# Scatters ahead of gathers in the expert loop of a mixture-of-experts layer on one Trainium2 core

## The chip, the cores and the metric

The kernel runs on one core of a Trainium2 chip. The time is the device time of one execution in microseconds (us). Engines: PE is TensorE, DVE is VectorE, ACT is ScalarE, POOL is GpSimd, and SP is SyncE, which here only issues DMAs and passes semaphores on. All engines run their own instruction lists in order and meet at semaphores.

## The reference

One transformer layer over 512 latent tokens of width 1024 with 256 context tokens: modulated normalisation, one input projection that feeds differential attention (4 heads) and a centred pooling group, an output projection, and then a mixture of experts. All of it is float32. The part that matters here is the last:

```python
scores = sigmoid(t @ w_router)                      # 512 tokens, 64 experts
wts, top_e = 8 experts per token (4 of 8 groups), weights normalised, times 2.5
yb = swiglu(x_of_slot, w_e_gate[e], w_e_up[e], w_e_down[e]) * slot_weight   # 1024 -> 256 -> 1024
routed = segment_sum(yb, slot_tok)                  # 8 rows per token
x = x + g_f * rmsnorm(routed + shared, g_post_ffn)
```

With the inputs drawn, the experts get between 1 and 265 tokens. In blocks of at most 64 tokens of one expert that makes 103 blocks; the first 62 experts (index 0 to 61) fill blocks 0 to 100, the expert with index 62 has block 101 and the last one block 102.

## The kernel before

**Stages.** Up to about 370 us the kernel does the layer's first half, the routing and the shared expert, and builds tables of which token stands in which slot. Then comes a loop over passes. A pass p takes two blocks of 64 slots (a pair, 128 rows), blocks 2p and 2p + 1. There are 52 passes; the count is computed at run time. At the end the four tiles of 128 tokens are summed, normalised and stored.

**What one pass needs.** Each step runs on another engine, and several passes are in flight:

- GpSimd gathers the pair's 128 token rows from DRAM into `xg[q]` (q is p % 2) with four indirect DMAs, 256 columns each (`gather`, L577, the DMA at L581). It takes its row indices from `gidx[:, q]`.
- VectorE turns the block, `turn_block` (L1756, instruction L1758), into `xT[:, q]`. It waits for the gather (`s_gt[q]`) and counts `s_xte`.
- TensorE multiplies with the gate and up weights, `gate_up` (L1274, 32 matmuls in two column halves of the array, one for each block of the pair). The second block's weights come from `cur_g`, which VectorE copies (`copy_gate_up`, L1754) once SyncE has counted the weights' arrival (`s_w`, L465).
- ScalarE applies SiLU (`block_silu`, L897), VectorE multiplies with the up half and the slot weights (`gated`, L1786), TensorE transposes the hidden rows (`turn_hidden`, L1297), VectorE keeps them (`keep_hidden`, L1792), TensorE multiplies with the down weights (`down`, L1286). The second block's down weights are a copy by ScalarE in `cur_d` (`copy_down`, L832).
- ScalarE copies the result out of PSUM into `ysb[:, q]` (`keep_y`, L893). For that it waits until the scatter of two pairs earlier, which read the same buffer, has landed (`s_scat[q]`).
- GpSimd scatters the 128 rows to DRAM with two indirect DMAs (`scatter`, L585): L588 writes rows, L591 adds rows to what stands there. It takes its indices from `sidx[:, q]`.

**Order on the engines.** TensorE in pass p: `turn_hidden` of p - 1, `gate_up` of p, `down` of p - 1. VectorE in pass p: turn the block of p + 1, `gated` of p, copy gate and up weights for p + 1, `keep_hidden` of p. ScalarE in pass p (`open_pass`, `close_pass`): the gather indices for p + 2 (`gather_index`, L834, behind a wait for the transpose of p), SiLU of p, `keep_y` of p - 1, the scatter indices of p - 1 (`scatter_index`, L838), `copy_down` for p. GpSimd in each step: the four gathers of p + 2, then the two scatters of p - 2. All six go through GpSimd's one DMA queue (q0).

**Weights.** SyncE loads one expert after the other (3 MB each) into a ring of 6 places (7 for the down weights), `load_gate_up` and `load_down`. Before a load it waits for the arrival of the expert two before it, and for the last matmul that uses the place (L524, L452).

**The end.** The last passes are written out. In them pass 50's `gate_up` follows `down` of 49. The last two pairs are not scattered: TensorE folds them into the tiles (`fold`, L1380) from `ysb`. When all scatters have landed, SyncE loads each tile's four partial sums (L542), VectorE adds them (`add_sums(t)`, three additions, L1825 to L1827), adds the folded rows (`add_rows`, L1851), and multiplies (`finish`, L1862 or L1865); ScalarE computes the norm in between (L955). In the last pass (k == -1) `add_sums(0)` stands in front of `keep_hidden`, whose copy the last `down` waits for.

Of the kernel before, what the change touches and what calls it, by code (L numbers as in the profile page):

```python
# [48 lines left out]
LEAST = E // 2  # L49
# [63 lines left out]
def build(nc, a, hbuf, sums, out):  # L113
    with ExitStack() as ctx:
# [82 lines left out]
        arow = rows[:, :].rearrange("p (r n) -> p r n", r=4)  # L197
# [31 lines left out]
        ysb = xres[:, 2:4, :]  # L229
# [324 lines left out]
        def _(pool):  # L554
# [22 lines left out]
            def gather(p, q, set_by):  # L577
                pool.wait_ge(s_gi, set_by)
                pool.sem_inc(s_pgo, 1)
                for s in range(4):  # L580
                    pool.indirect_dma_start(xg[q][:, 256 * s:256 * s + 256], None, hrows,  # L581
                                            bass.IndirectOffsetOnAxis(gidx[:, q, s:s + 1].bitcast(U32), 0),
                                            bounds_check=4 * T - 1, oob_is_err=False).then_inc(s_gt[q], 16)

            def scatter(p, q, rows_of_pair, indices_set):  # L585
                pool.wait_ge(s_si, indices_set)
                pool.sem_inc(s_pgo, 1)
                pool.indirect_dma_start(sums, bass.IndirectOffsetOnAxis(sidx[:, q, 0:1].bitcast(U32), 0),  # L588
                                        rows_of_pair, None, bounds_check=PARTS * T - 1, oob_is_err=False)\
                    .then_inc(s_scat[q], 16)  # L590
                pool.indirect_dma_start(sums, bass.IndirectOffsetOnAxis(sidx[:, q, 1:2].bitcast(U32), 0),  # L591
                                        rows_of_pair, None, bounds_check=PARTS * T - 1, oob_is_err=False,
                                        compute_op=ALU.add).then_inc(s_scat[q], 16)
# [15 lines left out]
            gather(1, 1, 1)  # L609
            pool.wait_ge(s_adre, 8)  # L610
            for p in range(2):
                gather(p + 2, p, p + 2)
                scatter(p - 2, p, arow[:, 3], p + 1)
            for t in range(NT):
                pool.wait_ge(s_sh_st[t], 16)
            pool.wait_ge(s_tab, 1)
# [1 line left out]
            more = pool.snap((extra + 3) // 4)  # L618
            last = pool.snap(more * 2 + (LEAST - 2))
            with pool.Fori(2, last, 2) as i:  # L620
                for q in range(2):
                    gather(i + (q + 2), q, i + (q + 2))
                    scatter(i + (q - 2), q, ysb[:, q], i + (q + 1))
            for q in range(2):
                n_set = pool.snap(more * 2 + (LEAST - 1 + q))
                scatter(None, q, ysb[:, q], n_set)
# [13 lines left out]
        def _(act):  # L640
# [184 lines left out]
            def down_weights(p):  # L825
                e = act.value_load(tab[0:1, bass.ds(p * 2 + 3, 1)], min_val=0, max_val=E - 1)
                return e, act.snap(((e + 1) % ND) * EW + 2 * CW)

            def copy_down(e, w0):
                act.wait_ge(s_wdn, e + 2)  # L830
                for j in range(FJ):
                    act.copy(cur_d[:, j, :], wring[:, bass.ds(w0 + j * D, D)]).then_inc(s_cdn, 1)  # L832

            def gather_index(p, q):  # L834
                act.wait_ge(s_xte, p - 1)
                act.copy(gidx[:, q, :], slot_g[:, bass.ds((p + 1) * 4, 4)]).then_inc(s_gi, 1)

            def scatter_index(p, q):  # L838
                act.copy(sidx[:, q:q + 1, :], slot_idx[:, bass.ds(p + 1, 1), :]).then_inc(s_si, 1)
# [50 lines left out]
            def keep_y(n, q, scattered):  # L890
                act.wait_ge(s_dn, n)
                act.wait_ge(s_scat[q], scattered)
                act.copy(ysb[:, q], pp[q]).then_inc(s_yev, 1)  # L893

            def block_silu(q, products):
                act.wait_ge(s_gu, products)
                act.activation(sg, pp[2][:, 512 * q:512 * q + F], ACT.Silu).then_inc(s_sil, 1)  # L897

            def open_pass(p, q):
                gather_index(p + 2, q)  # L900
                w = down_weights(p)
                block_silu(q, p + (NT + 1))
                return w

            def close_pass(p, q, w):
                keep_y(p + (NT + 1), 1 - q, p * 16 + 16 * q)
                scatter_index(p - 1, 1 - q)
                copy_down(*w)

            w = open_pass(0, 0)  # L910
            act.sem_inc(s_cdn, FJ)
            for n in range(1, NT):
                act.wait_ge(s_sh_st[n], 16)
            act.sem_inc(s_yev, 1)
            scatter_index(-1, 1)
            copy_down(*w)
            w = open_pass(1, 1)
            act.wait_ge(s_idx, 2)
            close_pass(1, 1, w)
            more = act.snap((extra + 3) // 4)  # L920
            last = act.snap(more * 2 + (LEAST - 4))
# [5 lines left out]
            def passes(k):  # L927
                return act.snap(more * 2 + (LEAST + k))

            def landed(k):  # L930
                return act.snap(more * 32 + 16 * (LEAST + k))

            w = open_pass(more * 2 + (LEAST - 4), 0)
            keep_y(passes(NT - 3), 1, landed(-4))
            scatter_index(more * 2 + (LEAST - 5), 1)
            copy_down(*w)
            w = open_pass(more * 2 + (LEAST - 3), 1)
            act.wait_ge(s_dn, passes(NT - 2))
# [464 lines left out]
        def _(dve):  # L1403
            order = [0]

            def then(ins):

                order[0] += 1
                ins.then_inc(s_cd, 1)
                dve.wait_ge(s_cd, order[0])  # L1410
# [64 lines left out]
            for g, w in enumerate(WINDOWS):  # L1475
                p = pT[:, g, :]
# [269 lines left out]
            def gate_up_weights(p):  # L1746
                e = dve.value_load(tab[0:1, bass.ds(p * 2 + 3, 1)], min_val=0, max_val=E - 1)
                return e, dve.snap(((e + 1) % NB) * EW)

            def copy_gate_up(e, w0):  # L1750
                dve.wait_ge(s_w, e + 2)
                w = wring[:, bass.ds(w0, 2 * CW)].rearrange("p (u k f) -> p u k f", u=2, k=KD)
                for k0, k1 in ((0, FIRST_KS), (FIRST_KS, KD)):
                    dve.tensor_copy(cur_g[:, :, k0:k1, :], w[:, :, k0:k1, :]).then_inc(s_cgu, 1)  # L1754

            def turn_block(q, gathered):  # L1756
                dve.wait_ge(s_gt[q], gathered)
                dve.transpose(xT[:, q].rearrange("p k (s r) -> p s k r", s=4),  # L1758
                              xg[q].rearrange("p (s r k) -> p s k r", s=4, k=KD)).then_inc(s_xte, 1)
# [20 lines left out]
            more = dve.snap((extra + 3) // 4)  # L1780
            last = dve.snap(more * 2 + (LEAST - 4))

            def gated(p, q, silus, turned):
                dve.wait_ge(s_sil, silus)
                dve.wait_ge(s_ht, turned)
                dve.scalar_tensor_tensor(hmid, sg, slot_w[:, bass.ds(p, 1)],  # L1786
                                         pp[2][:, 512 * q + F:512 * q + 2 * F], ALU.mult, ALU.mult).then_inc(s_hm, 1)

            def keep_hidden(q, turned, products):
                dve.wait_ge(s_ht, turned)  # L1790
                dve.wait_ge(s_dn, products)
                dve.tensor_copy(hTb, pp[3][:, 512 * q:512 * q + F].rearrange("p (j q) -> p j q", j=FJ))\  # L1792
                   .then_inc(s_hte, 1)
# [25 lines left out]
            def passes(k):  # L1819
                return dve.snap(more * 2 + (LEAST + k))  # L1820

            def add_sums(t):
                (p0, p1), (p2, p3) = ([h[:, 0:D], h[:, D:2 * D]] for h in parts[t])
                dve.wait_ge(s_yin[t], 32)
                dve.tensor_tensor(p0, p0, p1, ALU.add)  # L1825
                then(dve.tensor_tensor(p2, p2, p3, ALU.add))  # L1826
                then(dve.tensor_tensor(p0, p0, p2, ALU.add))  # L1827

            for k in range(-4, 0):
                q = k % 2  # L1830
                if k < -1:
                    e, w0 = gate_up_weights(more * 2 + (LEAST + 1 + k))
                    n_gathered = dve.snap(more * 64 + 32 * (LEAST + 2 + k + q))
                    turn_block(1 - q, n_gathered)
                gated(more * 2 + (LEAST + k), q, passes(NT + 1 + k), passes(NT + k))
                if k == -3:
                    keep_hidden(q, passes(NT + 2 + k), passes(NT + 1 + k))
                if k < -1:
                    dve.wait_ge(s_gu, passes(NT + 1 + k))
                    copy_gate_up(e, w0)  # L1840
                if k == -1:
                    add_sums(0)
                if k != -3:
                    keep_hidden(q, passes(NT + 2 + k), passes(NT + 1 + k))
                if k == -2:
                    owners()
# [10 lines left out]
            def finish(t):  # L1857
# [5 lines left out]
                else:  # L1863
                    dve.wait_ge(s_x1b, 16 * (NT - ADDED))
                    dve.scalar_tensor_tensor(y, parts[t][0][:, D:2 * D], frst[:, t:t + 1], x1b[:, t - ADDED, :],  # L1865
                                             ALU.mult, ALU.add).then_inc(s_fin, 1)

            add_sums(1)
            add_sums(2)
            add_rows(0)  # L1870
# [36 lines left out]
```

## Time and profile before

| | |
|---|---|
| median of 3 runs | 1007.27 us (1006.61 to 1007.97) |
| the profiled execution | 1007.2 us, its span 1005.4 us |
| mean granted TensorE clock | 0.984 |
| busy: PE, DVE, ACT, POOL | 93%, 52%, 33%, 46% of the span |
| the four gather DMAs (L581) | 208, 1233 ns each on GpSimd |
| the two scatter DMAs (L588, L591) | 50 each, 1225 and 1636 ns |
| keep_y (L893) | 52, 1012 ns each; idle before them 278.4 us |
| turning a block (L1758) | 52, 2046 ns each; idle before them 259.4 us |
| DMA | 299.69 MB, mean 298 GB/s over the span |

Times inside the profile count from the start of its span. A row of the timeline gives the start, the duration, the engine, the line, the operation with what it writes and reads, a count, and in brackets how long the engine was idle before it and what ended that. An "issue" there means that nothing which the profile shows was waited for. GpSimd's rows are the time to issue a DMA, not the time that its data take. A row `SPq` belongs to SyncE's queue.

### The profile page before, as it was taken

The page shows a single profiled execution, that of the slowest core. Times are in us where ns is not written, and L with a number is a line of the kernel's source. Part 1 is how long each engine was busy: PE and PEld are TensorE (multiplying, and loading weights), DVE is VectorE, ACT ScalarE, POOL GpSimd, SP SyncE. Part 2 cuts the span into 40 slices and gives each one's busy share as a digit, 9 for nine tenths or more (in the row PEclk, how much of TensorE's full clock was granted, in tenths as well). Part 3 has the DMA queues.
Part 4 walks back from the last instruction along what each step waited for, and adds up shares of the span by engine and source line. Part 5 has one row for each costly group of instructions (what it writes and reads, how often), then busy time and mean ns, then how long its engine had stood idle before and what let it go on. Part 6 is the DMA issues. An engine that isn't in the chain of part 4 may idle for free. (4 is left out here: it accounts for less than half of the span.)

```text
span 1005.4 us, 14543 instructions
## 1 busy us (share of the span) xinstructions
PE 938.9 (93%) x4307; PEld 405.4 (40%) x4308; DVE 520.6 (52%) x717; ACT 330.3 (33%) x591; POOL 462.3 (46%) x342
## 2 busy tenths in 40 slices
PE   3999999999999999999999989998999999989875
PEld 1644444677456543333333333332333333333322
DVE  1336779786267954444443444444444333444457
ACT  4212222576345412232232222332222233222322
POOL 0312432000000147666776775765776676766611
PEclk9999999999999999999999989998999999999978
DMA  9955442420325969999979999999999999999775
GB/s 371 355 206 209 168 178 94 187 119 1 139 83 199 388 241 354 397 398 389 395 287 404 408 398 388 402 395 378 407 361 358 382 366 379 365 368 349 214 290 154
DMA packets 68448, 299.69 MB, mean 298 GB/s; under 512 B 21518, under 2 KB 22514, under 8 KB 39361
## 3 DMA queue, kind: packets, MB, share of 16 engines
q1 hardware_dynamic: 41522, 261.16, 65.5%
q0 software_dynamic: 25840, 35.98, 13.6%
q10 hardware_dynamic: 1056, 2.18, 0.6%
q8 instruction: 14, 0.23, 0.1%
q14 instruction: 16, 0.13, 0.0%
HBM read 284.78 MB, written 62.91 MB: 346 GB/s over the span
## 5 line engine op out<-in xcount | busy, mean ns | idle before, releaser
L1274 PE MATMUL psum<-wring,xres 128*64 (+1 forms) x1664 | 373.8, 602 | 17.5 <-DVE wring L1754 16.1
L581 POOL DMA_INDIRECT xg<-h_rows,gidx x208 | 256.5, 1233 | 179.5 <-issue 92.7
L1758 DVE STREAM_TRANSPOSE xres<-xg 128x1024 f32<-128x1024 f32 x52 | 106.4, 2046 | 259.4 <-DMA xg<-h_rows,gidx 258.5
L1274 PEld LDWEIGHTS psum<-wring,xres 128*64 128x64 f32 x1664 | 120.7, 139 | 234.7 <-issue 234.6
L1286 PE MATMUL psum<-wring,rows 128*64 x416 | 189.7, 599 | 7.8 <-DVE rows L1792 6.9
L1286 PE MATMUL psum<-rows 128*64 128x512 f32 x416 | 189.7, 599 | 0.0
L893 ACT COPY xres<-psum 128x1024 f32<-128x1024 f32 x52 | 52.6, 1012 | 278.4 <-DMA expert_sums<-xres,sidx 238.9
L1754 DVE COPY wring<-wring 128x1536 f32 x104 | 123.0, 1224 | 16.1 <-SPq L465 14.6
L1286 PEld LDWEIGHTS psum<-wring,rows 128*64 128x64 f32 x416 | 57.4, 138 | 126.5 <-issue 126.5
L832 ACT COPY rows<-wring 128x1024 f32 x104 | 103.5, 1046 | 7.9 <-PE psum L1286 7.5
L591 POOL DMA_INDIRECT expert_sums<-xres,sidx x50 | 81.8, 1636 | 15.2 <-issue 15.2
L598 POOL TENSOR_TENSOR heads<-heads 128x512 f32<-128x512 f32 x4 | 5.1, 1269 | 169.4 <-DVE heads L1567 169.4
L1026 PE MATMUL psum<-actT,ring 128*128 128x512 f32 x192 | 82.6, 592 | 0.0
L572 POOL TENSOR_TENSOR ring<-ring 128x2048 f32<-128x2048 f32 x8 | 36.6, 4574 | 78.0 <-ACT ring L694 78.0
L588 POOL DMA_INDIRECT expert_sums<-xres,sidx x50 | 61.2, 1225 | 19.4 <-issue 15.3
L897 ACT ACTIVATE rows<-psum 128x256 f32<-128x256 f32 x52 | 20.0, 384 | 138.9 <-PE psum L1274 138.5
L1286 PEld LDWEIGHTS psum<-rows 128*64 128x64 f32 x416 | 57.4, 138 | 0.0
L1026 PEld LDWEIGHTS psum<-actT,ring 128*128 128x128 f32 x192 | 36.5, 190 | 45.5 <-issue 45.4
L1786 DVE SCALAR_TENSOR_TENSOR rows<-rows,slot_w,psum 128x256 f32<-128x256 f32 x52 | 23.6, 454 | 47.0 <-ACT rows L897 46.8
L1297 PEld LDWEIGHTS psum<-cst,rows 128*64 128x64 f32 x416 | 25.5, 138 | 40.5 <-issue 20.4
L1026 PE MATMUL psum<-ring,actT 128*128 128x512 f32 x96 | 41.8, 593 | 0.0
L694 ACT ACTIVATE ring<-ring,vec 128x2048 f32<-128x2048 f32 x8 | 16.0, 2002 | 73.7 <-DMA ring<-in_w_ada 73.7
(273 smaller groups left out, 919.8 us busy)
## 6 DMA issues: line engine op xcount, KB each, us to landing
wring<-in_w_e_gate SPq DMA_DIRECT2D x64, 1024.0 KB, 8.5
wring<-in_w_e_up SPq DMA_DIRECT2D x64, 1024.0 KB, 15.1
wring<-in_w_e_down SPq DMA_DIRECT2D x64, 1024.0 KB, 17.3
ring<-in_w_ada SPq DMA_DIRECT2D x20, 1024.0 KB, 5.2
wring<-expert_sums SPq DMA_DIRECT2D x8, 1024.0 KB, 11.7
ring<-in_w_in SPq DMA_DIRECT2D x3, 2048.0 KB, 25.7
heads<-in_w_ada SPq DMA_DIRECT2D x4, 1024.0 KB, 23.3
ring<-in_w_out SPq DMA_DIRECT2D x1, 4096.0 KB, 12.7
```

Of the source, the lines that this page charges most:

```text
L572: pool.tensor_tensor(part[:, 2048:], part[:, 2048:], wrow[1], ALU.add).then_inc(s_part[1], 1)
L581: pool.indirect_dma_start(xg[q][:, 256 * s:256 * s + 256], None, hrows, bass.IndirectOffsetOnAxis(gidx[:, q, s:s + 1].bitcast(U32), 0), bo ...
L588: pool.indirect_dma_start(sums, bass.IndirectOffsetOnAxis(sidx[:, q, 0:1].bitcast(U32), 0), rows_of_pair, None, bounds_check=PARTS * T - 1 ...
L591: pool.indirect_dma_start(sums, bass.IndirectOffsetOnAxis(sidx[:, q, 1:2].bitcast(U32), 0), rows_of_pair, None, bounds_check=PARTS * T - 1 ...
L832: act.copy(cur_d[:, j, :], wring[:, bass.ds(w0 + j * D, D)]).then_inc(s_cdn, 1)
L893: act.copy(ysb[:, q], pp[q]).then_inc(s_yev, 1)
L1026: last = pe.matmul(o, l, r, start=(k == 0), stop=(k == KD - 1))
L1274: last = pe.matmul(pp[2][SUB * g:SUB * g + SUB, 512 * q:512 * q + 2 * F] .rearrange("p (u f) -> p u f", u=2), xT[:, q, k, SUB * g:SUB * g ...
L1286: last = pe.matmul(pp[q][SUB * g:SUB * g + SUB, 512 * m:512 * m + 512], hTb[:, j, SUB * g:SUB * g + SUB], cur_d[:, j, 512 * m:512 * m + 51 ...
L1297: last = pe.matmul(pp[3][SUB * g:SUB * g + SUB, 512 * q + j * P:512 * q + (j + 1) * P], hmid[:, f0:f0 + 2 * SUB - j:FJ], ident, start=True ...
L1754: dve.tensor_copy(cur_g[:, :, k0:k1, :], w[:, :, k0:k1, :]).then_inc(s_cgu, 1)
L1758: dve.transpose(xT[:, q].rearrange("p k (s r) -> p s k r", s=4), xg[q].rearrange("p (s r k) -> p s k r", s=4, k=KD)).then_inc(s_xte, 1)
```

## The change

GpSimd issues the two scatters of a step ahead of the four gathers. ScalarE sets the gather indices one half round earlier: no longer at the start of a pass for the pair p + 2, but in the pass before, right behind the scatter indices and in front of the copies of down weights, for the pair p + 3. The first two are set in the prologue. VectorE's `add_sums(0)` moves from the last pass to behind it.

```diff
@@ gpsimd
             for p in range(2):
+                scatter(p - 2, p, arow[:, 3], p + 1)
                 gather(p + 2, p, p + 2)
-                scatter(p - 2, p, arow[:, 3], p + 1)
...
                 for q in range(2):
+                    scatter(i + (q - 2), q, ysb[:, q], i + (q + 1))
                     gather(i + (q + 2), q, i + (q + 2))
-                    scatter(i + (q - 2), q, ysb[:, q], i + (q + 1))
@@ scalar
             def open_pass(p, q):
-                gather_index(p + 2, q)
                 w = down_weights(p)
                 block_silu(q, p + (NT + 1))
                 return w
...
             def close_pass(p, q, w):
                 keep_y(p + (NT + 1), 1 - q, p * 16 + 16 * q)
                 scatter_index(p - 1, 1 - q)
+                gather_index(p + 3, 1 - q)
                 copy_down(*w)
 
+            gather_index(2, 0)
             w = open_pass(0, 0)
...
             scatter_index(-1, 1)
+            gather_index(3, 1)
             copy_down(*w)
...
             scatter_index(more * 2 + (LEAST - 5), 1)
+            gather_index(more * 2 + (LEAST - 1), 1)
             copy_down(*w)
@@ vector
-                if k == -1:
-                    add_sums(0)
                 if k != -3:
                     keep_hidden(q, passes(NT + 2 + k), passes(NT + 1 + k))
...
+            add_sums(0)
             add_sums(1)
             add_sums(2)
             add_rows(0)
```

`gather_index(p, q)` waits for `s_xte >= p - 1`, that is until the block p - 2, which stood in `xg[q]`, has been turned.

## Rows read from the trace of the kernel before

**Rows 1.** Stretches view: us, busy by engine, then TensorE clock, DMA share, GB/s

```profile
755.00:930.00 175.00, 166.47 (x846) 58.96 (x844) 75.36 (x76) 51.90 (x90) 119.05 (x90) 1.00 1.01 367
```

**Rows 2.** Timeline, TensorE's first matmuls of four passes: start, duration, instruction

```profile
701.03 7.04 PE L1274 MATMUL psum<-wring,xres 128*64 x32
...
711.76 7.04 PE L1274 MATMUL psum<-wring,xres 128*64 x32
...
929.04 7.09 PE L1274 MATMUL psum<-wring,xres 128*64 x32 [0.35 <-DVE wring L1754]
...
944.97 7.04 PE L1274 MATMUL psum<-wring,xres 128*64 x32
```

**Rows 3.** Waits view, 700 to 940 us: total, times, longest

```profile
ACT xres L893 <- DMA expert_sums<-xres,sidx: 134.0, 19, 9.3
```

**Rows 4.** Timeline of one round of the loop, 815 to 839 us

```profile
815.86 1.01 ACT L893 COPY xres<-psum 128x1024 f32<-128x1024 f32 x1 [6.91 <-DMA expert_sums<-xres,sidx]
...
816.86 1.99 ACT L832 COPY rows<-wring 128x1024 f32 x2
...
819.82 1.06 POOL L581 DMA_INDIRECT xg<-h_rows,gidx  x1 [2.02 <-ACT gidx L836]
...
822.68 2.36 DVE L1754 COPY wring<-wring 128x1536 f32 x2
...
824.06 1.86 POOL L581 DMA_INDIRECT xg<-h_rows,gidx  x1 [0.30 <-issue]
...
826.22 1.02 POOL L588 DMA_INDIRECT expert_sums<-xres,sidx  x1 [0.30 <-issue]
...
827.54 1.60 POOL L591 DMA_INDIRECT expert_sums<-xres,sidx  x1 [0.30 <-issue]
...
831.97 2.05 DVE L1758 STREAM_TRANSPOSE xres<-xg 128x1024 f32<-128x1024 f32 x1 [6.60 <-DMA xg<-h_rows,gidx]
...
835.45 7.09 PE L1274 MATMUL psum<-wring,xres 128*64 x32 [0.35 <-DVE wring L1754]
...
838.37 1.01 ACT L893 COPY xres<-psum 128x1024 f32<-128x1024 f32 x1 [7.02 <-DMA expert_sums<-xres,sidx]
```

**Rows 5.** Waits view of SyncE's queue, 525 to 940 us

```profile
SPq L452 <- PE psum L1274: 0.6, 2, 0.3
```

**Rows 6.** Source view of SyncE's line 465: two arrivals of gate and up weights

```profile
L465 SPq EVENT_SEMAPHORE  x1: 17/17/17, 686.8 to 686.8; - x1
...
L465 SPq EVENT_SEMAPHORE  x1: 17/17/17, 932.8 to 932.8; - x1
```

**Rows 7.** Timeline, TensorE after the arrival at 686.8

```profile
688.14 9.18 PE L1274 MATMUL psum<-wring,xres 128*64 x32 [4.66 <-DVE wring L1754]
```

**Rows 8.** Timeline: an unhindered keep, and the stage's longest gather

```profile
700.88 1.01 ACT L893 COPY xres<-psum 128x1024 f32<-128x1024 f32 x1 [3.13 <-PE psum L1286]
...
877.51 1.06 POOL L581 DMA_INDIRECT xg<-h_rows,gidx  x1 [2.27 <-ACT gidx L836]
...
891.03 2.04 DVE L1758 STREAM_TRANSPOSE xres<-xg 128x1024 f32<-128x1024 f32 x1 [7.33 <-DMA xg<-h_rows,gidx]
```

**Rows 9.** DMA view, 755 to 930 us, GpSimd's queue: packets, MB, share

```profile
q0 software_dynamic: 7210, 11.04, 24.8%
```

**Rows 10.** Timeline of the end of the kernel

```profile
969.29 1.23 DVE L1825 TENSOR_TENSOR wring<-wring 128x1024 f32<-128x1024 f32 x1 [5.04 <-DMA wring<-expert_sums]
...
973.93 1.11 PE L1286 MATMUL psum<-wring,rows 128*64 x1 [6.85 <-DVE rows L1792]
...
979.29 1.23 DVE L1825 TENSOR_TENSOR wring<-wring 128x1024 f32<-128x1024 f32 x1 [1.42 <-DMA wring<-expert_sums]
...
980.07 14.00 PE L1380 MATMUL psum<-xres 128*128 128x512 f32 x32
...
983.88 1.22 DVE L1851 TENSOR_TENSOR wring<-wring,psum 128x1024 f32<-128x1024 f32 x1 [0.97 <-PE psum L1380]
...
985.02 1.22 DVE L1825 TENSOR_TENSOR wring<-wring 128x1024 f32<-128x1024 f32 x1
```

## The prediction, made before the changed kernel ran

> **What bounds the kernel now.** The page's chain of waits holds only the last few per cent, so I went to the loop of 52 passes. First the stretches view: from 755 to 930 us the TensorE clock is full and the DMA engines are busy throughout (share 1.01) [rows 1]. Then TensorE's timeline: an undisturbed pass takes 10.73 us (701.03 to 711.76), but the 20 passes from 701.03 to 929.04 took 228.01, so 11.40 each: 13.4 us are lost there [rows 2]. The waits view names who is late: ScalarE's copy of a pair's result (L893) waited 134 us for the scatters, in 19 passes [rows 3].
>
> The timeline of one round shows why [rows 4]. ScalarE starts keep_y at 815.86; then come the scatter's indices, two copies of down weights and the gather's indices; only then does GpSimd start the four gathers (819.82), the last ends at 825.92, and only behind them go the two scatters (826.22, 827.54). They land when the next keep_y of that buffer starts, at 838.37. That closes a ring of 838.37 - 815.86 = 22.51 us for two passes, against 2 x 10.73 = 21.47 of TensorE's own. After a stall the ring has slack; it then slips about 1 us every two passes until TensorE waits.
>
> A second bound is the stream of expert weights. From 525 to 940 us SyncE waited for TensorE 0.6 us in all before a gate load [rows 5], so the loads run as fast as DMA lets them. By the routing of the reference's inputs the expert with index 62 opens block 101, the second block of pass 50 (counted from 0), and its gate and up weights are the last arrival that the view shows, at 932.8 [rows 6]. Pass 50 starts its gate_up at 944.97 [rows 2]. The same view shows what binding looks like: an arrival at 686.8, a gate_up at 688.14 after 4.66 us idle, and 9.18 us for its 32 matmuls where 7.04 is usual [rows 6, 7].
>
> **Scatter ahead of gather.** New round, from keep_y's start: today's gather starts 3.96 later (819.82 - 815.86). A scatter needs only its own indices, set before the two copies of down weights, and these take 1.99 of the 3.96 (the row at 816.86) [rows 4]; so the scatters start at about 2.0. They need 3.2 with their gaps (826.22 to 829.14, plus 0.3). They land 838.37 - 829.14 = 9.2 after issue. Ring: 2.0 + 2.9 + 9.2 = 14.1 us, well under 21.47; it stops binding. Saved: up to 13.4 us in the passes from 701 to 929.
>
> **The gathers' turn.** The four gathers now start 2.0 + 3.2 = 5.2 after keep_y, which starts 0.15 before a gate_up when nothing holds it (700.88 against 701.03) [rows 2, 8]: at 5.1 us into the pass. In the round shown they would be at 3.96 plus keep_y's own lateness, so the loop's worst passes gain and its best lose some 1.2. From the first gather to the transpose it lets go took 831.97 - 819.82 = 12.15, and from transpose to the gate_up of the pass behind it 835.45 - 831.97 = 3.48 [rows 4]. Two passes need at least 5.1 + 12.15 + 3.48 = 20.7, under 21.47, so hidden by 0.7. The longest such gather that I found in this stage took 891.03 - 877.51 = 13.52 [rows 8]: 22.1, or 11.05 a pass. I take 10.73 to 11.05 for passes; an equal gather costs nothing, the long one 0.3 a pass.
>
> One of GpSimd's issues takes longer where it meets VectorE's weight copy: the gather at 824.06 took 1.86 us beside the copy of 2.36 that began at 822.68, against 1.06 for the first [rows 4]. The reorder changes which issue is hit, not that one is: nothing in the sum. By the Trainium skill (SBUF — State Buffer, the warning on DVE blocking DMA under its port section) GpSimd can't write descriptors while such a copy holds the shared port; the row agrees. By it alone the sum is the same; were the copy to hit a scatter in place of a gather, the gathers would only gain 0.8 us of cover.
>
> **The earlier gather indices.** They are one 4-column copy, now in front of the down-weight copies: under 0.2 us, while TensorE starts the down matmuls only 7 us later. The move puts a wait for a transpose in front of these copies. Behind it queue the copies, the next SiLU, and for them TensorE's down and VectorE's gating. The transpose that the round at 838.37 would wait for began at 831.97 and takes 2; even with keep_y at 835.3 (0.15 before 835.45) the wait comes at 836.4, 2.4 us later. Cost 0. Without that cover each us beyond 4 would show in down. In the prologue the first scatter fills a gap and the second goes before the fourth block's gathers by 3 us, with a whole pass of cover: 0. On GpSimd the six issues are the same, nothing goes through SyncE's queue.
>
> **What the weights leave of it.** If passes run at 10.73, pass 49 starts at 701.03 + 214.7 = 915.7 and pass 50 (15.93 behind it today, in another order) at 931.6. But expert 62 arrives at 932.8 and its gate_up follows 1.3 later: 934.1. Moreover about one more pass of gathers and scatters then lies in front of it on the DMA engines. Their queue took 24.8% of 175 us [rows 9], over 15 passes 2.9 us each. So 937.0, at 8.0 us gain rather than 13.4; bounds 934.1 (no extra DMA) and 938.5 (half a pass more). TensorE then idles 3 to 5 us there, and by row 688.14 the matmuls behind lose 9.18 - 7.04 = 2.1 to the low clock level, or nothing if passes at 11.0 fill the time. Likely: 8.0 - 1.0 = 7.0. The passes before 701 are spaced by earlier arrivals like 686.8; I give them 0, bounds -0.5 and +1.
>
> **The first tile's sums later.** TensorE idles 6.85 until 973.93, since VectorE adds tile 0's sums (from 969.29, when they have landed) before it keeps the hidden block [rows 10]. That idle goes; down and the folds (980.07, 14.00 long) move up by about 5 to 8. But the end hangs on VectorE: tile 2's sums land at 979.29, whatever TensorE does, and behind them VectorE has its adds without a pause, except 0.97 before 983.88 where it waited for a fold. So 1.0 is saved; 0 if tile 3's sums land only at 985.02, 1.3 with small waits later. Tile 0's sums have landed at 969.29 and the hidden block is kept before that, so the moved adds displace nothing.
>
> Sum: 7.0 + 1.0 = 8.0. The profiled execution took 1007.2, its span 1005.4, the median of the runs 1007.27: forecast **999.3 us**.
>
> **The rivals.**
> *Passes at full rate, weights no bound* (15%). The weight loads don't slip and no clock is lost: pass 50 at 934.1 or sooner, gain 11 to 13 plus 1: 994. For it: pass 50's need is the only late one. Against: the DMA engines have no idle share [rows 1].
>
> *Gathers come later, yet no loss* (20%). They now follow the scatters at once, where today a pause of 2 or more lies between. If they land 1 to 2 us later, at 13.2 to 14.2, passes take 10.9 to 11.4, and the gain shrinks to between 0 and 7: about 1003. The Trainium skill (DMA: Bandwidth & Descriptors, section Queues, rings and completion order) says a ring's descriptors are consumed in order, which speaks for this one and the next.
>
> *Slower: gathers stand behind the scatters* (8%). If the gathers' data moves only when the scatters have landed: scatters end issue at 4.8 and land at 14.0 in the pass, gathers need the 831.97 - 825.92 = 6.05 they take today behind their last issue: 20.1, so 15.0 in place of 12.15. Two passes 23.6, one 11.8: 20 x 0.4 = 8 us slower, less 1.0: 1014. It turns to a loss when a gather takes over 22.8 - 8.6 = 14.2 us. Against: today's gathers, too, run with scatters in flight (826.22 to 838.37 spans the next gathers) and take 12.15.
>
> *The reorder does nothing* (7%). The scatters' landing, not their issue, takes what is gained, as all DMA is full: only the tail's 1.0 stays, 1006.2.
>
> **How the numbers follow.** My forecast has 50%, at 996.5 to 1002. The range for 8 in 10 takes in most of the first rival and the second: 994.5 to 1005. Under 0.2% (2 us) a measurement can't tell from no change. Faster: 50 + 15 + 14 of the 20 = 79%; the same: the other 6, the last rival's 7, so 13%; slower 8%.
>
> **What would show it.** Right: L893 waits for TensorE, not for scatters; first gather about 5 us after keep_y's start with the scatters ahead; passes after 701 at 10.7 to 11.1; an idle of 2 to 5 us ahead of pass 50 that ends on L465; the 6.85 gone, the last tiles' adds still pacing the end. Wrong: the transpose's wait for gathers growing past 14 us from the first issue; pass 50 before 934; or the weights' arrivals themselves moving, since all of it stands on 932.8.

## The result and the profile after

The changed kernel takes 1013.91 us (median of 8 runs, 1011.42 to 1016.47), the kernel before beside it 1008.06 (1006.02 to 1011.39, 8 runs): ratio 1.0042, 95% interval [1.0024, 1.006]. It became slower; the forecast was 999.3. The profiled execution took 1011.78 us, its span is 1009.9, which is 4.5 more than before.

The parts of these 4.5 us, read from the starts of TensorE's gate_up (the lines of gate_up, down and transpose are now L1277, L1289, L1761):

| stretch | before | after | difference |
|---|---|---|---|
| span's start to pass 0 | 372.64 | 372.90 | +0.3 |
| pass 0 to 29 | 328.39 | 332.94 | +4.6 |
| pass 29 to 49 | 228.01 | 227.32 | -0.7 |
| pass 49 to 50 | 15.93 | 18.12 | +2.2 |
| pass 50 to the end | 60.4 | 58.6 | -1.8 |

The forecast had put nothing in the second row and -7.0 in the third and fourth together. (Each column is one profiled execution. The first row, which the change hardly touches, lies between 371.4 and 375.1 us in the profiles of this case.) First, did the edit do on the engines what was said? One round of the loop after, to be held against [rows 4]:

```profile
817.14 1.01 ACT L893 COPY xres<-psum 128x1024 f32<-128x1024 f32 x1 [3.13 <-issue]
...
817.28 7.04 PE L1277 MATMUL psum<-wring,xres 128*64 x32
...
818.14 0.20 ACT L836 COPY gidx<-cst 128x4 int32 x1
...
819.12 1.02 POOL L588 DMA_INDIRECT expert_sums<-xres,sidx  x1 [2.18 <-ACT sidx L839]
...
820.44 1.59 POOL L591 DMA_INDIRECT expert_sums<-xres,sidx  x1 [0.30 <-issue]
...
822.34 1.07 POOL L581 DMA_INDIRECT xg<-h_rows,gidx  x1 [0.30 <-issue]
...
826.35 1.00 POOL L581 DMA_INDIRECT xg<-h_rows,gidx  x1 [0.30 <-issue]
...
828.44 7.09 PE L1277 MATMUL psum<-wring,xres 128*64 x32 [0.24 <-DVE wring L1757]
...
836.83 2.06 DVE L1761 STREAM_TRANSPOSE xres<-xg 128x1024 f32<-128x1024 f32 x1 [6.86 <-DMA xg<-h_rows,gidx]
...
839.08 1.01 ACT L893 COPY xres<-psum 128x1024 f32<-128x1024 f32 x1 [3.13 <-issue]
...
840.32 1.94 PE L1277 MATMUL psum<-wring,xres 128*64 x8 [0.35 <-DVE wring L1757]
```

It did. The first scatter goes 2.0 us behind keep_y's start, the first gather 5.06 us into the pass. But its rows let the transpose start only at 836.83: 14.49 us after the first issue, where the round of [rows 4] needed 12.15. With 3.49 to gate_up (840.32) the two passes take 23.04 us instead of 21.47. The waits view of 705 to 930 us (line, what it waited for: us in all, times, longest) says the same of the whole stage:

```profile
DVE xres L1761 <- DMA xg<-h_rows,gidx: 115.7, 18, 7.2
...
ACT xres L893 <- PE psum L1289: 47.0, 15, 3.1
```

The 134 us of waits for scatters [rows 3] are gone: keep_y no longer waits for a scatter anywhere in the loop. Yet the passes are as long as before, because the transpose's wait for gathers, which stood there before too (118.5 us in 19 times of the same stretch), now closes the ring. The stretches view shows an equally full DMA and hardly more work done in 175 us [rows 1]; the packets of GpSimd's queue take 25.4% of the 16 engines' time [rows 9]:

```profile
755.00:930.00 175.00, 168.96 (x858) 60.23 (x856) 75.70 (x76) 52.45 (x91) 106.04 (x94) 1.00 1.02 371
```

What was lost before pass 29 shows in the arrivals of weights. SyncE's waits from 500 to 530 us hold the one wait of TensorE's making, first before, then after:

```profile
SPq L452 <- PE psum L1274: 10.2, 1, 10.2
```

```profile
SPq L452 <- PE psum L1277: 12.9, 1, 12.9
```

That load (the expert with index 21) needs a ring place that pass 13 frees. Pass 13 began at 514.00 before and at 517.76 after. SyncE issues the load when the 32 matmuls of that pass's gate_up are done, first before, then after:

```profile
521.13 0.33 SPq L452 DMA_DIRECT2D wring<-in_w_e_gate  x1
```

```profile
524.88 0.33 SPq L452 DMA_DIRECT2D wring<-in_w_e_gate  x1
```

Its weights are there 8.3 and 7.5 us later, again before and after:

```profile
L465 SPq EVENT_SEMAPHORE  x1: 17/17/17, 529.4 to 529.4; - x1
```

```profile
L465 SPq EVENT_SEMAPHORE  x1: 17/17/17, 532.4 to 532.4; - x1
```

While SyncE waits for the place, the stream of weights pauses: the DMA share is 0.49 from 517 to 521 us before and 0.33 from 518 to 524 us after, where it is 1.0 in the late passes.

From there on SyncE waits for TensorE only 2.9 us more until 940, and the arrivals stay late: the one at 686.8 [rows 6] is now at 691.3, and the stall that it ends, [rows 7], is now this:

```profile
692.72 9.41 PE L1277 MATMUL psum<-wring,xres 128*64 x32 [5.54 <-DVE wring L1757]
```

The 2.2 us ahead of pass 50 are one late gather and the clock. Timeline of TensorE, VectorE and ScalarE, then stretches (TensorE's clock is the third number from the end):

```profile
942.00 2.05 DVE L1761 STREAM_TRANSPOSE xres<-xg 128x1024 f32<-128x1024 f32 x1 [7.31 <-DMA xg<-h_rows,gidx]
943.97 0.44 DVE L1789 SCALAR_TENSOR_TENSOR rows<-rows,slot_w,psum 128x256 f32<-128x256 f32 x1
...
944.47 0.66 PE L1300 MATMUL psum<-cst,rows 128*64 128x128 f32 x8 [0.79 <-DVE rows L1789]
...
946.10 0.64 PE L1289 MATMUL psum<-wring,rows 128*64 x1 [0.98 <-DVE rows L1795]
...
948.23 1.06 PE L1289 MATMUL psum<-wring,rows 128*64 x1
...
951.28 7.04 PE L1277 MATMUL psum<-wring,xres 128*64 x32
```

```profile
946.00:950.00 4.00, 3.90 (x12) 1.21 (x14) 1.87 (x2) 1.25 (x3) 1.57 (x2) 0.58 0.09 27
```

VectorE is still turning the late block when the SiLU of pass 49 is done, so gating, turn_hidden and down start late; after the idles of 0.79 and 0.98 us the granted clock is 0.58 on average over 4 us, so mostly the lower of its two levels (1.2 GHz, not 2.4), and a down matmul takes 1.06 us instead of 0.59. Before, the idles at this place were 0.29 and 0.97 us and the clock stayed full; from the first down matmul to pass 50 it took 3.48 us, and now 5.18, so the clock is 1.7 of the 2.2 us. These 2.2 us are not the order's: pass 49 to 50 takes 18.2 to 19.0 us, at a clock of 0.57 to 0.63, also in four of the six variants below that have early indices and gathers first there (e2, e4, e11, e15; not e10 and e14), and 16.0 to 16.3 at full clock in three that have scatters first (e1, e9, e13).

The end, beside [rows 10]:

```profile
973.43 0.64 PE L1289 MATMUL psum<-wring,rows 128*64 x1 [1.74 <-ACT rows L832]
...
975.10 1.23 DVE L1828 TENSOR_TENSOR wring<-wring 128x1024 f32<-128x1024 f32 x1 [2.94 <-DMA wring<-expert_sums]
...
977.01 14.00 PE L1383 MATMUL psum<-xres 128*128 128x512 f32 x32
...
980.14 1.23 DVE L1828 TENSOR_TENSOR wring<-wring 128x1024 f32<-128x1024 f32 x1 [1.42 <-DMA wring<-expert_sums]
```

TensorE's idle of 6.85 is 1.74, the folds start 3.1 earlier though pass 50 began 6.3 later, and VectorE's adds of the first three tiles are paced by the landing of the partial sums (each waits for them).

### The profile page after: what moved, and what is told of

It is laid out like the page before. It is cut to its first block and busy times, and to the rows that moved or that the text cites. A ratio compares the mean times of both kernels' runs of the same rounds, so it can differ in the third digit from the quotient of the medians.

```text
span 1009.9 us, 14543 instructions
## 1 busy us (share of the span) xinstructions
PE 936.0 (93%) x4307; PEld 404.2 (40%) x4308; DVE 522.7 (52%) x717; ACT 330.0 (33%) x591; POOL 423.0 (42%) x342
## 5 line engine op out<-in xcount | busy, mean ns | idle before, releaser
L1277 PE MATMUL psum<-wring,xres 128*64 (+1 forms) x1664 | 371.3, 599 | 21.7 <-DVE wring L1757 20.5
L581 POOL DMA_INDIRECT xg<-h_rows,gidx x208 | 226.8, 1090 | 88.3 <-issue 88.3
L1761 DVE STREAM_TRANSPOSE xres<-xg 128x1024 f32<-128x1024 f32 x52 | 106.5, 2048 | 277.4 <-DMA xg<-h_rows,gidx 270.6
L1277 PEld LDWEIGHTS psum<-wring,xres 128*64 128x64 f32 x1664 | 120.2, 138 | 237.8 <-issue 237.7
L1289 PE MATMUL psum<-wring,rows 128*64 x416 | 188.8, 597 | 2.7 <-ACT rows L832 1.7
L1289 PE MATMUL psum<-rows 128*64 128x512 f32 x416 | 188.8, 597 | 0.0
L588 POOL DMA_INDIRECT expert_sums<-xres,sidx x50 | 55.1, 1103 | 155.0 <-ACT sidx L839 86.3
L1289 PEld LDWEIGHTS psum<-wring,rows 128*64 128x64 f32 x416 | 57.2, 138 | 120.4 <-issue 120.4
L591 POOL DMA_INDIRECT expert_sums<-xres,sidx x50 | 80.6, 1611 | 15.2 <-issue 15.2
L1289 PEld LDWEIGHTS psum<-rows 128*64 128x64 f32 x416 | 57.2, 138 | 0.0
L1300 PE MATMUL psum<-cst,rows 128*64 128x128 f32 x416 | 32.5, 277 | 6.3 <-DVE rows L1789 4.4
```

Of the source, the lines that this page charges most:

```text
L1277: last = pe.matmul(pp[2][SUB * g:SUB * g + SUB, 512 * q:512 * q + 2 * F] .rearrange("p (u f) -> p u f", u=2), xT[:, q, k, SUB * g:SUB * g ...
L1289: last = pe.matmul(pp[q][SUB * g:SUB * g + SUB, 512 * m:512 * m + 512], hTb[:, j, SUB * g:SUB * g + SUB], cur_d[:, j, 512 * m:512 * m + 51 ...
L1300: last = pe.matmul(pp[3][SUB * g:SUB * g + SUB, 512 * q + j * P:512 * q + (j + 1) * P], hmid[:, f0:f0 + 2 * SUB - j:FJ], ident, start=True ...
```

## The experiments

Two theories at first. A: the gathers' data, right behind the scatters' in GpSimd's queue, come some 2 us later than before, and this alone makes the loss. B: an unwanted cost of the index move or of the sums, with the reorder neutral. C, added after the first runs: in the late passes DMA is full, and any order takes about the same.

**The three edits apart.** Each kernel has one or two of the change's edits.

```diff
# e1: gpsimd only            # e2: scalar only
+ scatter(...)               + gather_index(p + 3, 1 - q)   (close_pass)
  gather(...)                - gather_index(p + 2, q)       (open_pass)
- scatter(...)               # e3: vector only: add_sums(0) behind the last pass
                             # e4: e2 and e3 together
```

> Only the order on GpSimd is changed (scatters ahead of gathers); the gather indices and the first tile's sums stay where they were. Theory A (the scatters' data go ahead of the gathers' in GpSimd's one DMA queue, so each gather lands later): this edit alone carries the loss. The gather starts 5.2 us after keep_y as in the changed kernel, takes 13 to 16 us to the transpose in place of 12.2, pass 50 starts 5 to 7 us later than before, and without the sums edit the time is 1.5 us over the changed kernel's, 6 to 8 us over before. Theory B (ScalarE's new wait for a transpose and the earlier index copy cost it): no slower than before.

> Only the gather indices are set earlier, in front of the copies of down weights; GpSimd still issues gathers first. Theory A: the gathers start 2.0 us after keep_y and still take about 12.2 us; the scatters, behind them, start at 8.4 and land at 20.6 us after keep_y, under the 21.47 of two passes, so neither ring binds: passes from 701 us at 10.75 to 10.9, until pass 50 waits for its weights at 934 to 937 us. 6 to 9 us faster than before. Theory B: as slow as the changed kernel, 5 to 7 us over before.

> Only the first tile's sums are added later. Both theories: the loop is untouched, TensorE's idle time of 6.85 us before its last down matmuls shrinks to under 2, and the end moves by 1.0 to 1.8 us only, since VectorE's adds follow the landing of the sums.

> The early gather indices and the later sums together, GpSimd's order as before. Theory A: the two add up, 7 to 11 us faster than before. Theory B: 4 to 6 us slower.

Measured against the kernel before: e1 1.0054 [1.0033, 1.0074], e2 0.9968 [0.9952, 0.9983], e3 0.9995 [0.9978, 1.0012], e4 0.9963 [0.9947, 0.998]. So GpSimd's order alone is slower, the early indices alone are what gains, and the later sums can't be told from nothing. B falls. The sizes were missed: e2 gained some 3 us where 6 to 9 were expected and e4 some 4 where 7 to 11 were. Their gathers took 13.1 us, not 12.2, and late in the loop keep_y still waited for scatters (e2: 74.1 us in 11 passes between 705 and 930 us; before: 126.1 in 18), so passes 29 to 49 took 11.04 and not 10.75 to 10.9.

Where e1 loses is worth a look, since it differs from the kernel before in the order alone. From pass 0 to 28 it takes 320.2 us against 315.5, from 28 to 49 it takes 241.3 against 240.9: against the kernel before, the order costs in the early passes, and in the late ones one ring takes the place of another of the same length.

**No scatter data.** The changed kernel with both scatters' rows all out of bounds, so that they are issued but move nothing (the routed sums are left out of the output; the end loads one part of them four times).

```diff
- rows_of_pair, None, bounds_check=PARTS * T - 1, ...
+ rows_of_pair, None, bounds_check=0, ...
```

> The changed kernel, but both scatters of each pass drop their rows (all indices over 0 are out of bounds), and the end loads part 0 of the sums four times: the routed output is left out. GpSimd issues the same DMAs in the same order. Theory A (the gathers' data wait behind the scatters' of the same queue): the gather to transpose time falls from 14.5 us to 10 to 11 in the passes from 31 on and passes run at 10.74. Theory C (GpSimd's queue is a server with some 11.5 us of work per late pass beside the weights, and the order only sets who waits): the same, since the work itself is gone; under it the sum of both orders' latencies matters, and only e7 and e8 tell it from A. Rival D (the issue order or ScalarE's wait is to blame, not the data): latency and passes as in the changed kernel.

Measured: 978.05 us, a single run. Timeline of one gather, with keep_y and gate_up:

```profile
824.10 1.01 ACT L893 COPY xres<-psum 128x1024 f32<-128x1024 f32 x1 [3.13 <-PE psum L1289]
824.23 7.04 PE L1277 MATMUL psum<-wring,xres 128*64 x32
...
829.28 1.06 POOL L581 DMA_INDIRECT xg<-h_rows,gidx  x1 [0.30 <-issue]
...
834.97 7.04 PE L1277 MATMUL psum<-wring,xres 128*64 x32
...
840.65 2.05 DVE L1761 STREAM_TRANSPOSE xres<-xg 128x1024 f32<-128x1024 f32 x1 [5.04 <-DMA xg<-h_rows,gidx]
```

The gathers start just as late, 5.05 us into the pass, but are there 11.37 later, and every pass takes 10.74. The late start is no loss by itself; with the scatters' data it becomes one. They also leave the weights room: in 755 to 899 us the DMA share is 0.94.

**Less weight traffic.** In each order, 58 of the 64 loads of down weights are left out (later experts use old ones; the semaphore is counted up without a load).

```diff
 def load_down(n):
+    if n >= ND:
+        sp.sem_inc(s_wd[n % ND], 16)
+        return
```

> The changed kernel with only the first 7 down weights loaded (the other 58 loads left out, so the routed output uses stale weights): a third less weight traffic beside the same gathers and scatters. Theory C: with fewer packets of the other queue between its own, GpSimd's queue keeps up, the gather time falls under 12 us, passes run at 10.74. Theory A in its simple form (a fixed wait behind the scatters): still 14 to 15 us and passes of 11 to 11.5.

> The kernel before with the same 58 down loads left out. Theory C: the round from keep_y to keep_y falls under 21.47, late passes at 10.74, the same time as e7 but for the 1 to 2 us of the end. Theory A: late passes still 11.4 (a ring of 22.5 us made of issue times).

Measured, a single run each: 979.14 us in the new order, 976.2 in the old; passes 29 to 49 take 10.86 and 10.74, the DMA share in them is 0.80 and 0.79. With a third of the weights' traffic gone the ring of the scatters, on which the forecast had built, doesn't bind in the old order either, and the new order may still cost a little. The gathers take 11.0 us in the new order and 10.8 in the old. So the 2.3 us that the order adds to a gather in the late passes (e1 against before) are there only beside the full stream of weights.

**The adding scatter behind the gathers.** Plain scatter, gathers, adding scatter, in the loop.

```diff
-                    scatter(i + (q - 2), q, ysb[:, q], i + (q + 1))
+                    scatter_rows(i + (q - 2), q, ysb[:, q], i + (q + 1))
                     gather(i + (q + 2), q, i + (q + 2))
+                    scatter_add(i + (q - 2), q, ysb[:, q], i + (q + 1))
```

> The changed kernel, but in the loop the order is plain scatter, four gathers, adding scatter. Theory A: the gathers wait for one scatter only, their time is between 12.2 and 14.5 us (about 13.3), but the adding scatter starts 8.9 us after keep_y and lands 9 to 12 later, under or near 21.47: time between e4 and the changed kernel, 1006 to 1011. Theory C: late passes still 11.4 to 11.6, time 1007 to 1012. If the adding scatter alone holds the gathers up (read and write back), the latency falls to 12.2 and the time to e4's.

> The changed kernel with the adding scatter behind the gathers and the plain scatter ahead of them, again, beside the one above on the same chip. Its first result was 0.9935 with four runs. If it is really the best, it is 1 to 3 us under the one above, at 0.991 to 0.996; if late passes are bound by the transfers' sum whatever the order, both are equal within 0.2%.

> The gather indices early and the first tile's sums later, GpSimd's order as before: the same kernel as the earlier run of these two edits, beside the next one on the same chip. Again 0.995 to 0.998 of the kernel before, some 4 us.

Measured (e6, then e12): 0.9935 [0.9912, 0.9957] with 4 runs, but 0.9969 [0.9953, 0.9985] with 12 in the second job, beside e11 (the kernel of e4) at 0.9961 [0.9943, 0.9979]. The first was most likely the luck of four runs: e12 and e11 can't be told apart, and the gain of 0.3 to 0.4% is the early indices' own. The gathers take 14.5 us in e6 and e12 too, though only the plain scatter stands directly ahead; 13.3 or 12.2 was expected. But they start 3.2 to 3.4 us into the pass (median) in place of 4.85, so passes 29 to 49 take 11.20.

**Where in the loop the order costs.** My theory then was that the loss comes mainly from passes 4 to 13, by the ring place that pass 13 frees. The loop on GpSimd is split at its pass 14, with one order on either side.

```diff
-            with pool.Fori(2, last, 2) as i:
+            with pool.Fori(2, 14, 2) as i:    # e9, e13: gathers first; e10, e15: scatters first
+                ...
+            with pool.Fori(14, last, 2) as i: # the other order
```

The two passes ahead of the loop have scatters first in e9 and e10, gathers first in e13 and e15; e14 is e11 with scatters first in these two alone.

> The changed kernel, but GpSimd takes the gathers first in its passes before the 14th and the scatters first from the 14th on. If the scatters ahead of the gathers cost their time mainly in passes 4 to 13, by making the place for the next expert's weights come free later, then pass 13 begins near 514 us (changed kernel 517.8), pass 28 near 688 (692.7), the load that arrives at 691.3 arrives near 687, the later passes take 11.4 us as in the changed kernel, and the median is 3.5 to 5.5 us under the changed kernel, between 0.997 and 1.001 of the kernel before. If the loss arises in the late passes themselves, the median stays at 1.003 to 1.006.

> The mirror image: scatters first only in GpSimd's passes before the 14th, gathers first from then on. If the early passes carry the loss, pass 13 begins near 517.5 us and pass 28 near 692, as in the changed kernel, and passes 29 to 49 take 11.05 us as with early gather indices alone (changed kernel 11.37): a pass 49 near 926, and a median of 0.998 to 1.002. If the early order costs nothing that reaches the end, the median is that of the version with indices and sums, near 0.996.

> The version with scatters first from GpSimd's 14th pass on, with the first two passes, ahead of the loop, back to gathers first. Theory P (the first two scatters, which went ahead of the gathers in that version too, delay the weights' arrival for pass 6): that arrival falls back from 440.5 to about 437 us, passes 4 to 8 take 45.5 us in place of 48.3, pass 13 begins near 513.5, pass 28 near 688, and the median is 3 to 5 us under 1011.66. Theory L (what is lost comes from the late passes alone, the early difference was a chance of one profile): pass 28 moves, but the median stays within 1.5 us of 1011.66. In both, passes 28 to 49 take 240 to 242 us.

> The version with early indices and later sums, and scatters ahead of gathers in GpSimd's first two passes alone. Theory P: the arrival for pass 6 at 439 to 440.5 in place of 436.5, passes 4 to 8 at 48 us, pass 28 3 us later, median 3 us over 1003.4 to 1004.8. Theory L: median 1003 to 1005.

> Scatters first in GpSimd's passes 2 to 13 alone, with the first two and the later ones gathers first. Passes 8 to 13 take 56.5 us in place of 53.7 as in the other versions with scatters first there, pass 13 begins 3 us later, the load that waits for its place arrives 9.0 us behind it, and pass 28 is 3 us later. The median is 1005.5 to 1007.5 if these 3 us reach the end, 1003.4 to 1004.8 if the later stalls swallow them.

Measured, with the others for comparison. The columns with stretches are differences of gate_up starts in us, "gather" is the mean from a first gather's issue to the transpose that waited for it, in passes 31 to 49:

| kernel | scatters first in | 8 to 13 | 0 to 28 | 28 to 49 | gather | ratio |
|---|---|---|---|---|---|---|
| before | none, late indices | 54.2 | 315.5 | 240.9 | 12.2 | 1 |
| e11 | none | 53.7 | 315.8 | 234.3 | 13.2 | 0.9961 |
| e14 | first two | 53.7 | 316.5 | 234.8 | 13.3 | 0.998 [0.9963, 0.9996] |
| e15 | 2 to 13 | 57.1 | 319.7 | 234.0 | 13.1 | 0.9995 [0.9978, 1.0012] |
| e10 | 0 to 13 | 56.5 | 320.6 | 233.7 | 13.3 | 0.9995 [0.9984, 1.0007] |
| e13 | from 14 | 53.7 | 317.6 | 241.6 | 14.7 | 1.0025 [1.0002, 1.0048] |
| e9 | first two, from 14 | 53.7 | 318.8 | 242.4 | 14.6 | 1.0034 [1.0015, 1.0054] |
| after | all | 56.6 | 319.8 | 240.4 | 14.4 | 1.0042 |
| e12 | first two; in the loop the plain one alone | 53.8 | 318.9 | 235.0 | 14.5 | 0.9969 |

The early loss is as the theory had it, but it is the smaller half. Scatters first in passes 2 to 13 cost 3 us from pass 8 to 13 in each kernel that has both of them ahead; the weights behind the ring place then arrive some 15 us after pass 13's start (e11 512.98 and 528.7, e15 518.68 and 533.2), and pass 28 is 4 us later. (The 9.0 us that the expectation of e15 names are not an arrival: they are when SyncE, out of its wait, counts the load before this one, which before the change had landed at 516.6 already.) At the end this is worth 0.34% (e15 or e10 over e11; 0.15% over e14, which ran beside e15). Scatters first from pass 14 on cost 7 to 8 us between 28 and 49 and 0.64 to 0.73% at the end. The two halves add up to 1.0 to 1.1%, the whole order costs 0.8% over e11; with intervals of 0.2 to 0.3% on each this is no contradiction. C falls: with early indices the late passes take 6 to 8 us more in the one order than in the other. e9's miss (1.0034, where under 1.001 was expected) is this second half, which the comparison with the kernel before had hidden: before loses the same 7 us there to its late indices.

In e9 the stall at pass 6 was also longer, and pass 13 began at 518.7, not near 514. TensorE's idle there was 3.42 us, and the clock was 0.66 behind it:

```profile
442.00:447.00 5.00, 5.00 (x16) 1.48 (x16) 3.32 (x3) 0.00 (x0) 4.03 (x4) 0.66 0.98 370
```

Behind a shorter idle at the same place (2.08 in the changed kernel, 2.48 in e4) the next matmuls ran at full clock and the pass took 10.78 where e9's took 12.48. The length of the idle alone doesn't settle it: behind 3.34 us in e13 the clock stayed full, behind 3.28 in e10 it was 0.67. The first two scatters seem to have a part in this stall. The arrival that ends it comes 65.0 to 66.8 us (mean 65.8) after pass 0's start in the seven profiles with scatters first in passes 0 and 1, and 63.8 to 65.3 (mean 64.4) in the seven with gathers first there. Without scatter data (e5) it comes at 60.4. That is 1.3 us on average, with one profile for each kernel; e14's expectation had 2.5 to 4. e14 itself, at a median of 1006.14, lies between what its two theories wanted, and its interval overlaps e11's.

## Why the prediction was wrong

**The gathers' turn** is the step that failed: "an equal gather costs nothing". The gather was not equal. With scatters directly ahead it took 14.4 us on average in passes 31 to 49 instead of 12.2, beyond the largest that the prediction had found (13.52) and beyond the 14.2 at which it said that the gain turns. Its frame held: 5.1 + L + 3.48 for two passes gives 23.0, measured 23.04 in the round shown; and passes 29 to 49 took 11.37 each. The reason given against the slower rival was that gathers of before, too, run with scatters in flight and take 12.15. That was true, and misread. The next gather of the round in [rows 4] shows it (timeline of before):

```profile
831.24 1.06 POOL L581 DMA_INDIRECT xg<-h_rows,gidx  x1 [2.09 <-ACT gidx L836]
...
842.98 2.04 DVE L1758 STREAM_TRANSPOSE xres<-xg 128x1024 f32<-128x1024 f32 x1 [5.99 <-DMA xg<-h_rows,gidx]
```

The last scatter was issued until 829.14, the gather starts 2.10 later, and the transpose comes 13.84 us after 829.14. So I took, for passes 31 to 49 of each profile, the time from the end of the last scatter's issue to the transpose that waited for the gathers behind it: 14.6 before (mean pause 2.4 between the two issues) and 14.8 after (pause 0.3); in passes 8 to 13 14.0 and 14.3. Without scatter data it is 11.6. Two pairs differ in the order alone. From before to e1 the gather's own time grows by 2.3 us (12.2 to 14.5) and the time from the scatters' issue by 0.2 (14.6 to 14.8); from e11 to the changed kernel the first grows by 1.3 (13.2 to 14.4) and the second falls by 0.7 (15.5 to 14.8). So a pause of 2 us between the two issues costs the gathers' landing little or nothing: most of it is time that they would have waited anyway.

The packets in the traces point to the scatters' data as what they wait for. In GpSimd's queue, between the starts of passes 31 and 49, there are 1277 packets of 4096 bytes that take 310 to 340 ns before and 1374 after, but 10 without scatter data, so they are the scatters'. The last of them within 11 us of the scatters' issue starts 8.6 us behind it before and 9.2 after (medians of 19 rounds), and the transpose follows 5.8 and 5.5 us later, in no round less than 4.8. Whether the queue's order does it or its share of the full DMA engines, no run separates: e5 takes the scatters' packets and their traffic away together, and e7 and e8 change only the traffic beside them. The terms of the sum should have been 4.8 (scatters' end in the pass) + 14.7 + 3.5 = 23.0.

**Scatter ahead of gather.** Right in each step (scatters at 2.0, keep_y never waiting for a scatter), and worth nothing: the ring was replaced by the gathers' one. That it could be had in another way e2 shows: early indices alone bring passes 29 to 49 to 11.04. The prediction costed this edit at 0 and the reorder at all of the gain; it was the other way round. Early indices let the four gathers start 2.1 us behind keep_y instead of 3.96, and the scatters go that much earlier too. The scatters' ring still closes, but later: pass times stay at 10.7 to 10.9 up to pass 41 in e2, up to pass 33 before.

**"The passes before 701 are spaced by earlier arrivals ...; I give them 0, bounds -0.5 and +1"** failed as well, with +4.6. The arrivals aren't fixed: one load waits for a place that pass 13 frees (the waits of L452 above), passes 8 to 13 took 56.6 us instead of 54.2, and rows 5 began only behind that wait, at 525. From this load to the one that ends the stall at pass 28 it takes 157 to 159 us in all profiles with scatter data and all weights, so what is late at the first is late at the second.

**What the weights leave** was not put to the test: expert 62 arrived at 934.3, and pass 50 began 17 us later. (932.8 is expert 62's arrival, as the prediction says, but not the last in the trace: expert 63, which pass 51 needs, follows at 943.4.) Even in e11, pass 49 at 921.69, the arrival at 930.9 is 9 us ahead of pass 50 (939.89).

**The first tile's sums later**: 1.8 us less behind pass 50 in the profile, 1.0 expected; alone (e3), a ratio of 0.9995 whose interval holds both a gain of 1.0 us and none. Whether it gained anything is not shown.

**The rivals.** The one called slower had the sign and, with 1014, the time of 1013.91, but by other parts: it wanted 8 us in passes 29 to 49, where there are none against before, and none before 29. Measured against the right neighbour, the same kernel with gathers first (e4 or e11), it is there: 6 to 7 us in these passes. It wanted the gathers' data to move only when the scatters have landed, 15.0 us after the first issue and 20.1 into the pass; the round shown has 14.5 and 19.5. That is too near to tell it from a gather that is merely slower, and the packets above fit it. So the mechanism to which 8% were given is the likeliest one. The Trainium skill's rule of order within a ring (DMA: Bandwidth & Descriptors, section Queues, rings and completion order), quoted for this rival, agrees with e5 against the changed kernel (11.4 and 14.5 from the same start), with the reserve made above.

## What to carry to other kernels

Moving one transfer ahead of another in the same queue can make the second one later by more than the time to issue the first. Here its own time grew by 1.3 to 2.3 us besides. Count its landing from the issue of what stands ahead: a latency measured behind a pause may be short only because part of the waiting was done in the pause. Before an early stage is given nothing because arrivals space it, look for the one load that waits for a consumer. And when a change has several edits, ask of each what it would do alone: here one gained 0.3% and another lost 0.5%.

## What the hardware showed

Four gather DMAs took 12.2 us from first issue to use with a pause of 2.4 us behind the scatters and 14.4 right behind them (passes 31 to 49), which from the end of the scatters' issue is 14.6 and 14.8, with the weights' stream beside them; without scatter data it was 11.3 from first issue, and with a third of the weights away 11.0.

A clock below full came behind idles that are short. Ahead of pass 50, idles of 0.79 and 0.98 us were followed by a granted clock of 0.58 over 4 us; in e9, idles of 0.70 and 0.98 us at the same place left it full. At pass 6 single idles of 1.83 to 3.34 us left it full in nine profiles, while 3.28, 3.42, 3.68 and 5.0 us in e10, e9, e6 and e12 did not.
